# Row gathers issued a block earlier, four expert weight pieces requested in the output stage, and the down product moved ahead in further blocks, in a hybrid decoder step on one core

## What is computed

```
x = x + mixed @ w_out
h = rmsnorm(x, norm_ffn)
p_grp = softmax(h @ w_rg + b_rg)                     # 4 groups, the best one is taken
logit_in = (h @ w_re + b_re) of that group           # 8 experts, the best two are taken
weights = p_grp[best] * softmax(top two of logit_in)
y[token] += weight * (silu(h @ w_gate[e]) * (h @ w_up[e])) @ w_down[e]
return x + y
```

## Time and profile before

| | us |
|---|---|
| median of 3 runs (2529.76 to 2542.56) | 2537.25 |
| the profiled execution | 2536.91 |
| its span | 2535.2 |
| output stage | 1655 to 1826 |
| routing stage | 1826 to 1858 |
| expert stage, main loop | 1858 to 2476 |
| further blocks and the last scatters | 2476 to 2535 |

### The profile page before, as it was taken

One profiled execution on the slowest core, in us unless ns is written; L12 is line 12 of the kernel. 1 busy time (PEld: TensorE's weight loads), 2 busy tenths in 40 slices (PEclk: granted clock), 3 DMA queues, 4 the chain that ended last, 5 costly groups with the idle time before them and its releaser, 6 DMA issues. The chain is left out here.

```text
span 2535.2 us, 46962 instructions
## 1 busy us (share of the span) xinstructions
PE 2269.1 (90%) x20007; PEld 1625.7 (64%) x20007; DVE 764.3 (30%) x1601; ACT 509.1 (20%) x1413; POOL 447.1 (18%) x511
## 2 busy tenths in 40 slices
PE   8999998998779999779859999999669998898896
PEld 6446655887766666556646666644358887777775
DVE  2017342554456666434330000011231111111111
ACT  2211111332115555433200000001101111111110
POOL 1044120222220111210210000011102211221112
PEclk9999999999559999899979999999879999999998
DMA  5000300000400000275471100022289999999992
GB/s 176 34 34 33 133 11 1 2 2 17 91 1 1 1 2 1 62 190 159 124 200 51 33 34 34 0 86 91 101 320 354 364 351 351 354 355 353 354 370 79
DMA packets 153836, 336.54 MB, mean 133 GB/s; under 512 B 33807, under 2 KB 81432, under 8 KB 153422
## 3 DMA queue, kind: packets, MB, share of 16 engines
q1 hardware_dynamic: 131830, 305.97, 34.7%
q0 software_dynamic: 13632, 21.44, 3.6%
q10 hardware_dynamic: 8160, 6.07, 0.8%
HBM read 316.70 MB, written 44.55 MB: 142 GB/s over the span
## 5 line engine op out<-in xcount | busy, mean ns | idle before, releaser
L2552 PE MATMUL psum<-f_W,f_xT 128*32 128x384 f32 x3264 | 369.5, 499 | 46.8 <-DMA f_W<-w_up 45.9
L2554 PE MATMUL psum<-f_W,f_xT 128*32 128x128 f32 x3264 | 374.2, 278 | 0.0
L2554 PEld LDWEIGHTS psum<-f_W,f_xT 128*32 128x32 f32 x3264 | 361.3, 112 | 2.7
L2083 PE MATMUL psum<-hT,x_wg 128*128 128x344 f32 x768 | 229.0, 457 | 4.2 <-DMA x_wg<-w_in 4.2
L400 PE MATMUL psum<-w,hT 128*128 128x512 f32 (+1 forms) x512 | 202.4, 553 | 0.0
L2083 PEld LDWEIGHTS psum<-hT,x_wg 128*128 128x128 f32 x768 | 147.4, 192 | 81.6 <-DMA x_wg<-w_in 4.3
L2552 PEld LDWEIGHTS psum<-f_W,f_xT 128*32 128x32 f32 x3264 | 149.2, 111 | 52.0 <-issue 39.6
L400 PE MATMUL psum<-hT,w 128*128 128x344 f32 x576 | 169.1, 454 | 0.0
L400 PEld LDWEIGHTS psum<-w,hT 128*128 128x128 f32 x512 | 97.3, 193 | 96.8 <-issue 89.5
L1620 ACT ACTIVATE a_P<-psum,a_nmax 128x512 f32<-128x512 f32 (+4 forms) x256 | 123.1, 494 | 125.8 <-DVE a_nmax L1538 85.6
L400 PEld LDWEIGHTS psum<-hT,w 128*128 128x128 f32 x576 | 108.6, 190 | 57.1 <-ACT dnT L451 0.9
(11 more groups left out here) (521 smaller groups left out, 3655.7 us busy)
## 6 DMA issues: line engine op xcount, KB each, us to landing
f_W<-w_gate SPq DMA_DIRECT2D x34, 2048.0 KB, 21.1
f_W<-w_up SPq DMA_DIRECT2D x34, 2048.0 KB, 28.6
f_W<-w_down SPq DMA_DIRECT2D x34, 2048.0 KB, 27.7
k_stage<-cache_nsa SPq DMA_DIRECT2D x128, 192.0 KB, 2.5
w<-w_in SPq DMA_DIRECT2D x6, 2048.0 KB, 8.1
x_wg<-w_in SPq DMA_DIRECT2D x8, 1024.0 KB, 11.3
x<-x_prompt SPq DMA_DIRECT2D x8, 512.0 KB, 5.7
o_w<-w_out SPq DMA_DIRECT2D x2, 2048.0 KB
```

Of the source, the lines that this page charges most:

```text
L2083: ins = nc.tensor.matmul(PS[b + i][:, 0:n], wg[q % 3][:, k, i, c:c + P], hT[:, k, t0:t0 + n], start=(k == 0), stop=(k == KD - 1))
L2552: nc.tensor.matmul(PS[bank][row[t], 0:NQ], xT[par][:, k, row[t]], m[:, k, 0:NQ], start=(k == 0), stop=(k == KD - 1))
L2554: ins = nc.tensor.matmul(PS[bank][row[3], P * t:P * t + P], xT[par][:, k, row[t]], m[:, k, NQ:FE], start=(k == 0 and t == 0), stop=(k == K ...
```

## The change

**Weight pieces.** The three sets of buffers f_W become nine pieces of 16 KB per partition, each with a place of its own from A_PIECE on. x1 and h2p of the output stage move to other places. SP asks for gate, up and down of expert 0 and for gate of expert 1 in the turns t = 2 to 5 of the output stage, behind the h2 store of the turn. The routing stage asks for the five others.

**Gathers.** In GpSimd's main loop scatter(b - 1) becomes scatter(b - 2), while gather(b + 2) stays, so that a gather comes a block earlier relative to the scatters. Two scatters then stand behind the loop.

**Further blocks.** PE does down(b) ahead of transpose_rows(b + 2), and ACT and DVE copy in that order.

The core of the diff (imports of names, signatures and the order of two calls in build are left out):

```diff
-A_W = A_R + (NT + 1) * D * 4
+A_PIECE = A_R + 128
...
-        Z = Region(L, A_R, A_R + 32768)
-        x1 = Z("o_x1", [P, 3, D])
+        load_gate, load_up, load_down = weights[5:]
+        x1 = L.at("o_x1", A_OB + 4096, [P, 3, D])
+        h2p = L.at("o_h2p", A_PIECE + 32768, [P, 2, D])
+        Z = Region(L, A_RS, A_PIECE + 65536)
+        zrow = Z("o_zero", [1, D])
...
                 if t >= 1:
                     store(sp, t - 1)
+                if t in (2, 3, 4, 5):
+                    (load_gate, load_up, load_down, load_gate)[t - 2](sp, t // 5, t // 5)
             store(sp, NT)
...
-    W = [L.at(f"f_W{i}", A_R + 49152 * i, [P, 3 * 4096]) for i in range(3)]
-    wg, wu = ([w[:, o:o + 4096].rearrange("p (k n) -> p k n", k=KD) for w in W] for o in (0, 4096))
-    wd = [w[:, 8192:12288].rearrange("p (k n) -> p k n", k=4) for w in W]
+    piece = lambda name, i, k: L.at(f"f_{name}", A_PIECE + 16384 * i, [P, k, 4096 // k])
+    wg, wu = ([piece(name, i, KD) for i in at] for name, at in (("wg", (0, 7, 5)), ("wu", (1, 2, 6))))
+    wd = [piece("wd", i, 4) for i in (4, 3, 8)]
...
         @block.sync
         def _(sp):
-            for e in range(3):
-                load_gate_and_up(sp, e, e)
-                load_down(sp, e, e)
+            load_up(sp, 1, 1)
+            load_down(sp, 1, 1)
+            load_gate(sp, 2, 2)
+            load_up(sp, 2, 2)
+            load_down(sp, 2, 2)
...
             for b in range(NE):
                 pool.wait_ge(xt_done, b + 1)
                 gather(b + 2)
-                if b >= 1:
-                    scatter(b - 1)
+                if b >= 2:
+                    scatter(b - 2)
+            scatter(NE - 2)
             scatter(NE - 1)
...
                 scatter(b)
+                pool.wait_ge(x_loaded[b % 2], 16 * (b // 2 + 2))
                 pool.wait_ge(stored[b % 2], 32 * (b // 2 + 1))
-                pool.wait_ge(x_loaded[b % 2], 16 * (b // 2 + 2))
...
             def each(b):
                 gate_and_up(b, b % 3, b % 2, b // 3 + 1)
                 transposes(b)
+                down(b, b % 3, b // 3 + 1)
                 transpose_rows(b + 2, b % 2, b // 2 + 2)
-                down(b, b % 3, b // 3 + 1)
```

More of the change, by code:

```diff
@@ L2111, in _, with block_out @@
                 nc.gpsimd.tensor_tensor(mixed[m][:, t0:t0 + n], sg[u % 2][:, 0, 0:n], sg[u % 2][:, 1, 0:n], ALU.add).then_inc(m_done, 1)
-def block_out(nc, L, PS, C, x_p, x_s, norm_ffn, w_rg, w_re, b_rg, b_re, mixed, wo, wo_loaded, h2_rows, logits, y_p, y_s):
+def block_out(nc, L, PS, C, weights, x_p, x_s, norm_ffn, w_rg, w_re, b_rg, b_re, mixed, wo, wo_loaded, h2_rows, logits, y_p, y_s):
     ctx = ExitStack()
@@ L2134, in block_out @@
         bias = Z("o_bias", [P, NG + NE])
-        h2p = Z("o_h2p", [P, 2, D])
         by_row = lambda x: x.rearrange("p (k j r) -> p k r j", k=KD // 2, r=2)
-        zrow = Z("o_zero", [1, D])
         ss, mean, r = Z("o_ss", [P, 16]), Z("o_mean", [P, 16]), Z("o_r", [P, 16])
@@ L2267, in expert_weights, with load_rows, load_gate, load_up @@
     gu_loaded, d_loaded = ([sem(n + str(i)) for i in range(3)] for n in ("gu_loaded", "d_loaded"))
-    W = [L.at(f"f_W{i}", A_R + 49152 * i, [P, 3 * 4096]) for i in range(3)]
-    wg, wu = ([w[:, o:o + 4096].rearrange("p (k n) -> p k n", k=KD) for w in W] for o in (0, 4096))
-    wd = [w[:, 8192:12288].rearrange("p (k n) -> p k n", k=4) for w in W]
+    piece = lambda name, i, k: L.at(f"f_{name}", A_PIECE + 16384 * i, [P, k, 4096 // k])
+    wg, wu = ([piece(name, i, KD) for i in at] for name, at in (("wg", (0, 7, 5)), ("wu", (1, 2, 6))))
+    wd = [piece("wd", i, 4) for i in (4, 3, 8)]
     of = lambda w, e: w[bass.ds(e, 1)]
-    def load_gate_and_up(queue, i, e):
-        for dst, w in ((wg[i], w_gate), (wu[i], w_up)):
-            queue.dma_start(dst.rearrange("p (k r) n -> p k (r n)", r=2), of(w.rearrange("e (k p r) n -> e p k (r n)", p=P, r=2), e).rearrange("a p k n -> (a p) k n")).then_inc(gu_loaded[i], 16)
+    def load_rows(queue, dst, w, i, e):
+        queue.dma_start(dst[i][:, :, :].rearrange("p (k r) n -> p k (r n)", r=2), of(w.rearrange("e (k p r) n -> e p k (r n)", p=P, r=2), e).rearrange("a p k n -> (a p) k n")).then_inc(gu_loaded[i], 16)
+    def load_gate(queue, i, e):
+        load_rows(queue, wg, w_gate, i, e)
+    def load_up(queue, i, e):
+        load_rows(queue, wu, w_up, i, e)
     def load_down(queue, i, e):
-        queue.dma_start(wd[i], of(w_down.rearrange("e (k p) n -> e p k n", p=P), e).rearrange("a p k n -> (a p) k n")).then_inc(d_loaded[i], 16)
-    return wg, wu, wd, gu_loaded, d_loaded, load_gate_and_up, load_down
+        queue.dma_start(wd[i][:, :, :], of(w_down.rearrange("e (k p) n -> e p k n", p=P), e).rearrange("a p k n -> (a p) k n")).then_inc(d_loaded[i], 16)
+    return wg, wu, wd, gu_loaded, d_loaded, load_gate, load_up, load_down
 def block_route(nc, L, PS, C, logits, weight, tokens, slot_weight, blocks, weights):
@@ L2293, in block_route @@
             sem, ("step", "exp_in", "exp", "a_ready", "rank", "iota", "iota_ready", "hot_ready", "table", "weights_copied"))
-        load_gate_and_up, load_down = weights[5:]
+        load_gate, load_up, load_down = weights[5:]
         Y = Region(L, A_HT, A_CONST)
@@ L2453, in block_experts @@
         sem = L.signals.named("f_")
-        wg, wu, wd, gu_loaded, d_loaded, load_gate_and_up, load_down = weights
+        wg, wu, wd, gu_loaded, d_loaded, load_gate, load_up, load_down = weights
         xt_done, xT_act, xT_dve, gu_done, silu_done, prod_done, a_done, at_done, aT_done, down_done, out_act, out_dve, gidx_ready, sidx_ready, scattered = map(
@@ L2484, in load @@
                 sp.wait_ge(gu_done, b - 2)
-                load_gate_and_up(sp, w, e)
+                load_gate(sp, w, e)
+                load_up(sp, w, e)
                 sp.wait_ge(down_done, b - 2)
@@ L2627, in each @@
                 silu(b)
+                copy_out(b, b % 2, b // 2 + 1)
                 copy_rows(b + 2, b % 2)
-                copy_out(b, b % 2, b // 2 + 1)
             further(act, each)
@@ L2735, in build @@
     h2_rows = nc.dram_tensor("h2_rows", [TT + 1, D], F32, kind="Internal").ap()
-    block_out(nc, L, PS, C, I["x_prompt"], I["x_sample"], I["norm_ffn"][0], I["w_router_g"][0], I["w_router_e"][0],
+    weights = expert_weights(L, I["w_gate"][0], I["w_up"][0], I["w_down"][0])
+    block_out(nc, L, PS, C, weights, I["x_prompt"], I["x_sample"], I["norm_ffn"][0], I["w_router_g"][0], I["w_router_e"][0],
               I["b_router_g"][0], I["b_router_e"][0], mixed, wo, wo_loaded, h2_rows, logits, O["y_prompt"][0], O["y_sample"][:, 0])
-    weights = expert_weights(L, I["w_gate"][0], I["w_up"][0], I["w_down"][0])
     block_route(nc, L, PS, C, logits, weight, tokens, slot_weight, blocks, weights)
```

## The result

The changed kernel takes 2519.54 us (median of 6 runs, 2514.70 to 2525.37) against 2535.04 for the kernel before in the same comparison (6 runs, 2529.76 to 2542.56). The ratio is 0.994 with a 95% interval of 0.9921 to 0.9959: 15 us less, between 10 and 20. The forecast was 12.2 us less and 2525.0 us; the measured time lies in the range of 2517 to 2533.

A forecast was written before the change was run, and what follows sets the result against it. The weight stream was taken to bound the expert stage's middle, its start held by block 0. From 2537.25 us, 5.1 at the head and 7.1 in the further blocks gave 2525.0, with a range of 2517 to 2533.

The forecast's parts named there:

- The likeliest case: Whole kernel: both gains, at the head and in the further blocks, come in; 2518 to 2532 us, chance 0.80.
- Part 1, the head: Start of the expert stage: first gathers meet empty DMA engines, gate and up of block 0 start 5.1 us earlier.
- I take 2.1 + 1.3 = 3.4 us: First gathers: landing on empty engines, as an empty gather's 2.1 us plus 1.3 for moving the rows.
- The chain behind it: Head: from gather 0's landing through transposes and copy to gate and up of block 0, at 1865.8 instead of 1870.93.
- The pieces in the output stage cost nothing: Output stage: four weight pieces on SP's queue, 5.5 us each, hidden by PE's projection; cost 0.
- Rival 3: Output stage: pieces landing 28.6 us after issue delay four x tiles, 13.6 us, total 2538.6; chance 0.04.
- Part 2, gathers a block ahead: Main expert loop: PE had no wait for rows in the middle, so the gain is 0.
- Part 3, the further blocks: Blocks 32 and 33: down product no longer waits for gather 34; gate and up of block 33 start 7.1 us earlier.
- that fall of the clock: Block 32: if the clock falls for gather 34's transposes and about 1 us of the next product, the gain is 5.4.
- Rival 2: Tail: GpSimd's scatters 30, 31 and gather 34 end 7 us later, so the tail gives nothing, 2532.1; chance 0.06.

The follow-up runs named there:

- e9: The changed kernel with the gathers' edit undone: 2521.58 us, ratio 0.9942 to the kernel before.
- e10: The changed kernel again, nothing altered: 2521.22 us, ratio 0.9943 to the kernel before.
- e2: The kernel before with only the gathers a block ahead: 2532.18 us against 2535.26, ratio 0.9988.
- e6: The kernel before with only the gathers a block ahead, measured a second time: 2529.65 us against 2534.20, ratio 0.9981.
- e7: The kernel before against itself, as a control: 2533.64 us against 2534.20, ratio 0.9993.
- e5: The kernel before with only the new places in SBUF, all nine pieces requested in routing: 2530.14 us against 2534.20, ratio 0.9986.
- e12: The kernel before with the new places in SBUF and the gathers a block ahead: 2531.84 us against 2534.38, ratio 0.9984.
- e8: The changed kernel with the further blocks in the main loop's order and gather 34 not issued: 2512.43 us, ratio 0.9922 to the kernel before.
- e3: The kernel before with only the new order in the further blocks: 2529.28 us against 2535.26, ratio 0.997.
- e4: The changed kernel with the last three routing pieces held until the slot table is done: 2521.96 us in its one run.

## Why the prediction was right, and where it was not

**The sum.** Forecast 5.1 + 7.1 = 12.2 us, measured 15.5 and 13.2 by medians. The likeliest case came in, a little beyond the bound of 0.5% to which I had given 0.41. The number owes something to luck: the two forecast parts brought 3.7 + 7.1 = 10.8 us, and the rest came from the middle, for which the sum had no term.

**Part 1, the head: the mechanism was right, the size was too large.** I had 5.1 us from a landing of 3.4. Measured are 4.0 in the profile of the changed kernel, and 24.6 − 20.9 = 3.7 in the mean over the kernels of the table. The step that was mis-sized is "I take 2.1 + 1.3 = 3.4 us": a full gather on empty engines lands in 4.0 to 4.6 us, 4.1 in the median. The 2.1 us of an empty gather plus the time of the bytes falls 0.7 short. The Trainium skill, page "DMA: Bandwidth & Descriptors", section "Anatomy of one DMA — SWDGE (gpsimd) path", has a fit that gives, as an estimate, 2.9 us, and the trace's 4.1 doesn't agree with it. The chain behind it was right: gather 1 was no longer a wait, the transposes of block 1 waited 0.74 us for the copy of the rows of block 0. With 4.1 in place of 3.4 the same chain gives 4.4 (measured 12.18 − 7.91 = 4.3), and from the start of gate and up of block 0 to load number 3 it took 12.87 us, not 12.64, so that 0.2 was given back.

**The pieces in the output stage cost nothing**, as forecast. SP's first load of routing comes 170.5 us after its first load of the output stage, as before (1655.58 to 1826.03, and 1657.48 to 1827.95). The x tiles land in 6.8 us in the median, not 4.2, and no DMA of their buffers took over 9.4 us, of the 29.4 they have:

```profile
o_x<-x_prompt SPq DMA_DIRECT2D x8, 512.0 KB, 6.8
...
f_wd<-w_down SPq DMA_DIRECT2D x1, 2048.0 KB, 8.5
```

Rival 3 needed a piece that lands 25.2 us after its issue; it lands in 8.5.

**Part 2, gathers a block ahead: nothing, as forecast, in the changed kernel** (e9 against e10). In the kernel before it gave 3.1 and 4.6 us (e2, e6), which the forecast's 0 doesn't cover. See the open point.

**Part 3, the further blocks: right.** 7.1 us forecast, 6.7 in the profile of the changed kernel, 7.1 over the table, although the clock fell in four of the five kernels of that mean. In e10 the chain went as written: PE waited 0.98 us for gather 34 (I had 1.1), and gate and up of block 33 started 7.2 us behind the copy of aT (I had 7.4). In the changed kernel's profile the product took 7.06 us, its first 3.3 us at a granted clock of 0.51, where I had put 5.4 at full clock; the wait for the gather vanished behind it, and 1.6 − 1.1 = 0.5 us remained as a loss. I had priced that fall of the clock with the gather's wait; it comes, when it comes, with the idle time ahead of the down product, before the gather matters. Rival 2 did not come: gather 34 was issued 4.2 us behind the copy of aT, before 4.4 (2493.43 − 2489.01), and GpSimd stood ready for scatter 32 and 33 until ACT had copied the results.

**What the forecast missed is the middle.** It is 586.6 to 588.5 us in the three profiles with both old places and old gathers, and 582.3 to 585.8 in all eleven others. The two sets don't overlap, and the difference of the means, 587.8 − 584.2 = 3.6 us, is what the head (3.7) and the end (7.1) leave of the measured 13 to 15.5. It is no matter of where the border to the end lies: with the old order in the further blocks, middle and end together are 651.6 and 652.6 us in before and e7, and 647.2 to 649.9 in the five others. It builds up along the stream: the gate weights of block 12 are requested 159.8 to 162.5 us behind load number 3 in all fourteen, with the three in between, and the last gate load comes after 569.9 to 572.3 us in the three and 565.4 to 569.2 in the eleven. But I have no mechanism. The bytes, the loads' order and the full engines are the same; new places alone and gathers alone each bring it, and both together bring no more. In the four comparisons of these edits (e2, e5, e6, e12) the whole interval lies below 1, in two by only 0.0001, and in the control it doesn't. With three profiles on one side chance is unlikely, but not excluded. **This stays open.**

## What to carry to other kernels

A small indirect transfer whose result starts a stage should not go out into a full weight stream: ask for the weights a stage earlier (or hold back those that are not needed first, which no run here tried). When every byte has to come through full engines anyway, such a shift is worth only what it brings at the start of the stream, here 3.7 of 2535 us. The bandwidth-bound middle doesn't take it back: it is 582.3 to 585.8 us in the kernels with the early head, and 583.1 to 588.5 in the others. In a loop's rare last blocks look for a wait on work that nobody needs; and the main loop's order, with a product of the block before to cover the other engines, is worth keeping there too (about 5 us in e8, together with the gather that is left out).

## What the hardware showed that I had not expected

The first gathers, 96 rows of 4 KB each, land in 4.1 us in the median on empty engines (4.0 to 4.6) and in 8.1 (7.6 to 9.2) beside a stream of 2 MB loads. The medians of one program differ by 0.6 us between two sets of 12 and 29 runs, while single runs spread over 17 us (2525.33 to 2542.46), so that an edit worth 3 us can hardly be told from nothing by one comparison. And after the same idle times the granted clock fell to 0.50 or 0.51 in the changed kernel, e3 and e4 and stayed at 1.00 in e10, the same program as the changed kernel: 1.6 us on one product.
